# A two-layer decoder trunk on one core: the 32 loads of the first layer's scale and shift are issued by GpSimd instead of SyncE

## The reference

```python
mod = silu(c) @ w_ada + b_ada                 # c is one row of 2048; w_ada is 2048 x 6144
shift, scale, gate = split(mod, 3)
h = rmsnorm(x, norm_pre) * (1 + scale) + shift
z = h @ w_in                                  # 2048 x 14336: gb, gcin, u, g_c, q, k, v, g_r
y_conv = gb * causal_conv3(gcin * u) * silu(g_c)
q, k = rope(q, positions), rope(k, positions) * dk ** -0.5
y_ret = groupnorm(retention(q, k, v)) * gn_gain * silu(g_r)
o = concat(y_conv, y_ret) @ w_out             # 4096 x 2048
x = x + gate * rmsnorm(o, norm_post)
```

## Time and profile before

| | |
|---|---|
| median of 3 runs | 1730.23 us (1729.31 to 1730.43) |
| profiled execution | 1728.81 us, span 1727.0 us |
| TensorE busy | 1685.4 us, 98% |
| VectorE busy | 1161.1 us, 67% |
| ScalarE busy | 719.5 us, 42% |
| GpSimd busy | 51.0 us, 3% |
| moved by DMA | 429.25 MB, mean 249 GB/s |

### The profile page before, as it was taken

How to read it: one execution, slowest core, us unless ns; L and a number is a source line. 1 busy time by engine, 2 the same in 40 slices (tenths; PEclk the granted TensorE clock), 3 DMA queues, 4 the chain that set the end, 5 groups by cost and what they waited for, 6 DMA issues and landing times. The chain is left out here.

```text
span 1727.0 us, 18943 instructions
## 1 busy us (share of the span) xinstructions
PE 1685.4 (98%) x7707; PEld 1376.3 (80%) x7707; DVE 1161.1 (67%) x1296; ACT 719.5 (42%) x802; POOL 51.0 (3%) x94
## 2 busy tenths in 40 slices
PE   6999999999999999999999999999999999999997
PEld 3567878888888888778878888888888888888886
DVE  2788767788578868777776456556555654567776
ACT  3344444434444444343455444444434444444332
POOL 4000000000000000000000000000000000000000
PEclk9999999999999999999999999999999999999999
DMA  9998655787788769877775666567556756668774
GB/s 341 383 383 316 211 180 191 271 293 263 253 289 312 270 217 323 321 274 284 282 248 164 197 203 196 189 196 219 193 178 202 216 187 189 209 242 303 290 286 179
DMA packets 233655, 429.25 MB, mean 249 GB/s; under 512 B 8664, under 2 KB 50024, under 8 KB 232800
## 3 DMA queue, kind: packets, MB, share of 16 engines
q1 hardware_dynamic: 225888, 408.97, 68.5%
q10 hardware_dynamic: 7680, 19.07, 4.0%
HBM read 417.57 MB, written 2.10 MB: 243 GB/s over the span
## 5 line engine op out<-in xcount | busy, mean ns | idle before, releaser
L809 DVE TENSOR_TENSOR w_lo<-stage,w_hi 128x1024 fp32r<-128x1024 f32 x574 | 692.9, 1223 | 467.2 <-ACT w_hi L588 464.5
L588 ACT CAST w_hi<-stage 128x1024 fp32r<-128x1024 f32 x574 | 595.7, 1051 | 945.6 <-PE Z L1275 576.2
L1273 PE MATMUL Z<-w_hi,H 128*128 128x512 f32 x1784 | 702.6, 394 | 11.0 <-DVE w_lo L809 6.4
L1275 PE MATMUL Z<-w_hi,H 128*128 128x512 f32 x1784 | 695.6, 390 | 0.0
L1274 PE MATMUL Z<-w_lo,H 128*128 128x512 f32 x1784 | 695.1, 390 | 0.0
L1273 PEld LDWEIGHTS Z<-w_hi,H 128*128 128x128 f32 x1784 | 335.3, 188 | 88.9 <-issue 8.0
L1275 PEld LDWEIGHTS Z<-w_hi,H 128*128 128x128 f32 x1784 | 335.3, 188 | 70.7
L1274 PEld LDWEIGHTS Z<-w_lo,H 128*128 128x128 f32 x1784 | 335.5, 188 | 67.9
L830 DVE SCALAR_TENSOR_TENSOR acc<-stage,c_silu,acc 128x512 f32<-128x512 f32 x240 | 180.2, 751 | 6.8
L1273 PE MATMUL Z<-w_hi,YR 128*128 128x512 f32 x256 | 100.2, 391 | 2.8 <-DVE w_lo L809 2.8
L1273 PE MATMUL Z<-w_hi,YC 128*128 128x512 f32 x256 | 99.7, 389 | 0.0
(11 more groups left out here) (160 smaller groups left out, 735.0 us busy)
## 6 DMA issues: line engine op xcount, KB each, us to landing
stage<-in_w_in SPq DMA_DIRECT2D x186, 1024.0 KB, 5.2
stage<-in_w_ada SPq DMA_DIRECT2D x64, 1024.0 KB, 7.4
stage<-in_w_out SPq DMA_DIRECT2D x64, 1024.0 KB, 7.4
stage<-in_w_in SPq DMA_DIRECT2D x74, 512.0 KB, 5.6
front_stage<-in_w_ada SPq DMA_DIRECT2D x32, 1024.0 KB, 11.2
behind<-R ACTq DMA_DIRECT2D x14, 448.0 KB, 3.5
taps<-in_conv_w ACTq DMA_DIRECT2D x18, 256.0 KB, 6.5
xt<-in_x SPq DMA_DIRECT2D x2, 1024.0 KB, 6.7
```

The source lines that it names most:

```text
L588: N.copy(w_bufs(n, h)[0], stage[:, slot_of(n), 2 * h:2 * h + 2, :]).then_inc(s_hi, 1)
L809: V.tensor_tensor(lo, stage[:, slot_of(n), 2 * h:2 * h + 2, :], hi.bitcast(F32), ALU.subtract)\
L1273: T.matmul(z[:, i, :], hh, wh, start=ch.first and a == 0, stop=False)
L1275: ins = T.matmul(z[:, i, :], hl, wh, start=False, stop=stop)
```

## The change

GpSimd issues the 32 front loads on its own queue, by a new function `front_loads(upto)`, which issues the front loads up to a number, each when its slot is free. It is called at three points of GpSimd's program: for the first 4 at the start, for the next 8 after the first 1/rms, and for the other 20 after the angles. SyncE skips them in its list. Tiles, sizes, slots, semaphores and the instructions of the other engines are the same.

```diff
             for what in LOADS:
                 kind, n, kc = what
-                ring, i = RINGS[kind == "front"], PLACE[what]
+                if kind == "front":
+                    continue
+                ring, i = RINGS[False], PLACE[what]
                 slot = i % SLOTS
                 if i >= SLOTS:
                     was, m, k = ring[i - SLOTS]
                     if was == "w":
                         sp.wait_ge(s_lo, HALVES[m + 1])
-                    elif was == "front":
-                        sp.wait_ge(s_fv if on_vector(m, k) else s_front, front_done(m, k))
...
-                if kind == "front":
-                    k0, tiles = FRONT_GROUPS[n // 2]
-                    at, rows_ = front_rows_of(n, kc)
-                    col = (1 - n % 2) * D + k0 * P
-                    src = w_ada[0, at * P:(at + rows_) * P, col:col + tiles * P].rearrange("(a p) n -> p a n", p=P)
-                    sp.dma_start(front_tile(n, kc)[0], src).then_inc(s_fstage[slot], 16)
-                elif kind == "ada":
+                if kind == "ada":
...
+            def front_loads(upto):
+
+                for i in range(loaded[0], upto):
+                    _, n, kc = RINGS[True][i]
+                    if i >= SLOTS:
+                        _, m, k = RINGS[True][i - SLOTS]
+                        pool.wait_ge(s_fv if on_vector(m, k) else s_front, front_done(m, k))
+                    k0, tiles = FRONT_GROUPS[n // 2]
+                    at, rows_ = front_rows_of(n, kc)
+                    col = (1 - n % 2) * D + k0 * P
+                    src = w_ada[0, at * P:(at + rows_) * P, col:col + tiles * P].rearrange("(a p) n -> p a n", p=P)
+                    pool.dma_start(front_tile(n, kc)[0], src).then_inc(s_fstage[i % SLOTS], 16)
+                loaded[0] = upto
+
+            loaded = [0]
+            front_loads(SLOTS)
             step(G.memset(mhalf[:, :], -0.5))
             rstd(1, slice(NT, 2 * NT))
+            front_loads(3 * SLOTS)
             ang, u, m = (wide(R2)[:, i * NT * HALF:(i + 1) * NT * HALF] for i in range(3))
             pool.wait_ge(s_pos, 16 * NT)
             pool.wait_ge(s_par, 16 * 10)
...
             step(G.tensor_scalar(ang, ang, edge, None, ALU.min))
             step(G.tensor_scalar(ang, ang, -edge, None, ALU.max))
             pool.sem_inc(s_ang, 1)
+            front_loads(len(RINGS[True]))
             pool.wait_ge(s_sin, 2)
```

## The result

| | before | after |
|---|---|---|
| median | 1730.33 us (4 runs, 1729.31 to 1731.41) | 1745.9 us (4 runs, 1744.35 to 1747.43) |
| ratio after to before | | 1.0091, 95% interval 1.0076 to 1.0106 |
| profiled execution | 1728.81 us, span 1727.0 | 1746.72 us, span 1744.9 |

A forecast was written before the change was run, and what follows sets the result against it. TensorE is busy 98%; in the front, 30 to 114 us, the DMA engines are full. The 13th front tile's delay, +16.6, less 4.2 and 0.7 us, gives +11.7; median 1741.9, stated as 1741, range 1734 to 1749 us.

The forecast's parts named there:

- The start, +2 us: First product, at 30.08 us before: weight loads in flight beside the first front tiles delay it by 2 us.
- The angle block on the path: GpSimd's 32 angle instructions, 21.1 us plus 2 us stretching, run before the 13th front load and delay it.
- The issue, 0.5 us: GpSimd's issue of the 12th front load before the angle block, taken at SyncE's median of 0.518 us.
- The landing, 5.8 us: The 13th front load, issued at 72.1 us after the angles, lands 5.8 us later, at 77.9.
- f12 16.6 us late: TensorE multiplies the 13th front tile, at 61.30 us before, only when it lands at 77.9: 16.6 us late.
- What is given back, 4.9 us: TensorE's earlier idle time shrinks after the stall: 4.2 us back in 61 to 92 us, 0.7 in 92 to 114.
- The low clock, 0 us: The low-clock stretch at 92 us, costing 1.7 us, moves behind the new stall at the same price: 0.
- The steady part, 0 us: Front stretch: weight loads running ahead and front tiles coming later cancel, 0, bounds -7.0 and +5.5 us.
- The cosine step: GpSimd's cosine step, now after the last front load, has tables ready about 155 us, needed at 190.03: no cost.
- The faster one: Rival: weight loads freed from 47 us of front waits save 8.7 us, giving 1721.5 us; chance 0.07.
- The issue of 4.1 us: Rival: each front load costs GpSimd 4.1 us to issue, giving 1749 us; chance 0.10 beyond 1748.
- That the queues do nothing new: Rival: all loads share the same 16 DMA engines, so without the angle block no stall; no chance given.

The follow-up runs named there:

- kernel 6: The kernel before with only the first four front loads issued by GpSimd, the other 28 by SyncE: 1730.88 us against 1730.79.
- kernel 2: The changed kernel with GpSimd issuing only the first 12 front loads and SyncE the other 20 as before: 1731.21 us against 1730.26 for the kernel before.
- kernels 3 and 4: The changed kernel with one round of the angle reduction instead of three, 1736.92 us, and with six rounds, 1762.58 us; kernel before 1730.26.
- kernel 12: The changed kernel without the 27 instructions of the angle reduction, the other 5 before the first 1/rms: 1732.47 us against 1731.02 for the kernel before.
- Kernel 5: The changed kernel with 32 unused TensorE products before the wait for the 13th front tile: 1745.42 us against 1730.79 for the kernel before.
- kernels 1: The changed kernel with the 32 angle instructions spread behind the 8th to 13th front load: 1732.91 us against 1730.26 for the kernel before.
- kernel 7: The changed kernel, seven angle instructions before the first 1/rms, others spread behind the 8th to 12th load, first weight load waiting for the second front tile: 1732.22 us, ratio 1.0011.
- 8: The changed kernel, seven angle instructions before the first 1/rms, others spread behind the 8th to 12th load, no added weight-load wait: 1733.21 us against 1730.79 before.
- kernels 9 and 11: The changed kernel, angle instructions spread, SyncE keeping its old front-slot waits: 1734.63 us; also with weight loads waiting for the second front tile: 1736.12; kernel before 1730.38.

## Why the prediction held, point by point

*What bounds the kernel.* Right: the front, and in it the DMA engines. TensorE's idle time after 180 us is the same in both kernels (18.4 and 18.5 us). But the lateness was not settled at 114 us, as the prediction had it: it was 13.2 us there and 15.6 at the cosine step.

*The start, +2 us.* The first product starts at 32.33 us instead of 30.08, +2.25. That the delay enters the end only through the angle block was not tried by itself, but kernel 6, with a start 1.4 us late and no load behind the block, lost nothing.

*The angle block on the path.* Right, and the cause: kernel 2 takes the loads away from behind it and is as fast as before; kernels 3 and 4 change its length and move the time with it. It took 23.5 us; 21.1 + 2 had been taken. Behind it lay a gap of 0.60 us that I had not counted.

*The issue, 0.5 us.* An issue takes 0.75 us on GpSimd. The summary of the line (duration of an issue in ns, minimum, median and maximum, then the time to landing in us):

```profile
L1185 POOL DMA_DIRECT2D front_stage<-in_w_ada x32: 748/750/1107, 1.2 to 159.1; - x32
...
DMA to landing us min/median/max: 5.6/10.1/21.2
```

It is longer than SyncE's median of 0.518 but it is never 4.1. The end of f11's issue came at 49.84 us instead of 49.0.

*The landing, 5.8 us.* 79.61 - 73.95 = 5.66 us.

*f12 16.6 us late.* It was 18.3. The difference is 0.84 (end of f11's issue) + 0.4 (block) + 0.6 (gap) - 0.14 (landing) = 1.7 us. TensorE's idle time for it is 16.17 us, where the prediction had named 10 to 15.

*What is given back, 4.9 us.* By the front tile of 113.65 us the delay had shrunk from 18.3 to 13.2 us, so 5.1 came back, nearly what was predicted. Then it grew by 2.4 us up to the cosine step, in a stretch where nothing had been idle. This is the line from TensorE's waits between 114 and 180 us:

```profile
PE Z L1285 <- DVE part L1016: 1.7, 3, 0.7
```

So net 2.7 us were given back instead of 4.9. The prediction had closed its account at 114 us, and in the window from 114 to 180 us the loads are still being caught up with, 344 GB/s where 311 had been. Why 2.4 us are lost there was not tried by itself. It need not come from the stall: kernel 12, which has none, loses 2.1 us in the same stretch.

*The low clock, 0 us.* The stretch at a mean granted clock of 0.52 lasted 6.4 us, 3.1 us of lost clock instead of 1.7, so 1.4 us more. Kernel 5 undid most of that and is only 0.5 us less late at the cosine step, so on the end 0 was about right.

*The steady part, 0 us.* Not a gain, rather a loss of 1.4 to 2.7 us: all kernels that have the 32 loads on GpSimd and no block (1, 7, 8, 12) lose that much. It is small: it is below the 0.2% that the prediction calls the least that can be told from no change, and the lower ends of the four intervals are 1.0002 to 1.0006. Kernels 2 and 6, with 12 and 4 loads on GpSimd, lose less (ratios 1.0002 and 1.0). In kernel 12 it arises between 114 and 190 us, and the reason stays open. It is not a late issue of GpSimd at f13; kernels 9 and 11 do not settle whether it is the order of the weight loads; and the larger packets on GpSimd's queue, 8704 where SyncE's queue had 20992, were not tried by themselves. In the change itself this rest is not to be told from the block's effect.

*The sum.* In the terms of the prediction: +18.3 - 5.1 + 2.4 = +15.6 us at the cosine step, against 15.6 by the medians and 11.7 predicted. The terms that were too small are f12's delay (1.7 us) and what happens after 114 us (2.4 us, put at nothing). The profiled executions differ by 17.9. Of the other 2.3 us 1.6 are the clock near 260 us: both kernels have the same idle time of 2.51 us in TensorE's timeline there (first fence of before, second of after), but only after the change does a stretch at a low granted clock follow, 3.4 us long (last fence; before, the granted clock is 1.00 from 240 to 256 us):

```profile
244.06 0.50 PE L1273 MATMUL Z<-w_hi,H 128*128 128x512 f32 x1 [2.51 <-DVE w_lo L809]
```

```profile
259.67 0.70 PE L1285 MATMUL Z<-w_hi,H 128*128 128x512 f32 x1 [2.51 <-DVE w_lo L803]
```

```profile
259.60:263.00 3.40, 3.33 (x8) 2.65 (x9) 3.40 (x5) 0.00 (x0) 0.00 (x0) 0.53 0.27 67
```

Kernels 2 and 6, which are level with before by their medians, show it too (granted clock 0.89 from 240 to 256 us). So I take it for the spread of single executions and not for an effect of the change.

*The cosine step.* It ran at 159.84 us, and the tables are needed only some 205 us after the start; no cost, as said.

*The rivals.* The faster one (weight loads that no longer stand behind front waits) is refuted without the block as well: kernels 1, 7, 8 and 12 have the unblocked queue and no block, and none gains (1.0011 to 1.0015). The half of it that was true is that ScalarE's waits for weights fell, from 45.4 to 30.5 us between 30 and 114 us in kernel 12; nothing came of it at the end. The issue of 4.1 us did not come (0.75). That the queues do nothing new is true of the queues and misses the block. The Trainium skill ("DMA: Bandwidth & Descriptors", section "Issuing engines are not separate DMA queues") says that transfers started from different engines share the same 16 DMA engines and that a further issuing engine saves only issue time. The runs agree: 382 GB/s with one queue and at most 382 with two, from 30 to 114 us. The page "SBUF — State Buffer" of the Trainium skill ("Who interferes with whom") has VectorE, in its two-port modes, lock GpSimd out of writing descriptors. No run here shows it: GpSimd's issues took 0.75 us beside a busy VectorE and 1.1 us at most. In which mode VectorE worked beside them the rows do not say.

## What to carry to other kernels

A load that is moved to another engine's queue stands behind all work of that engine, so look at what is long there and compare it with how far ahead the loads run: here 23.5 us of arithmetic, begun at 49.8 us, stood before a tile that TensorE could use at 62.5 (kernel 2). In a stretch where the DMA engines are full, do not count idle time that TensorE had before as a store that a stall draws on for good: 5.1 us came back by 114 us here, and only 2.7 in the end. The transfer time missing at the rate of the stretch gave the loss to within 3 us in all thirteen kernels. A second queue gained nothing here, where the first already kept the DMA engines full; if loads must be on such an engine, cut its other work into portions between them (13 of the 15.6 us came back), or leave on the old queue those that come behind it (all of it came back).

## What the runs showed of the hardware

- GpSimd issues a load of 1 MB in 0.75 us with hardly any spread (0.748 least, 0.750 median); the first ones took up to 1.107 us. SyncE's took 0.367 to 4.102 us for the same tiles. No issue of GpSimd's took several us, though the DMA engines were as full.
- The same 33.56 MB were 20992 packets on SyncE's queue and 8704 on GpSimd's.
- A few small loads of ScalarE's queue came 3 us later after the change. TensorE's first instruction that needs them starts at 14.32 us; before, at 11.08 (second fence). SyncE's weight loads go out earlier too; when the first of them waits for f1 (kernel 7), it starts at 13.22:

```profile
14.32 0.72 PE L1380 MATMUL Z<-ident,R 80*128 80x80 f32 x3 [14.32 <-DMA R<-in_conv_w]
```

```profile
11.08 0.72 PE L1368 MATMUL Z<-ident,R 80*128 80x80 f32 x3 [11.08 <-DMA R<-in_conv_w]
```

- After 16.17 us of idle time TensorE worked at a mean granted clock of 0.52 (mostly at 1.2 GHz instead of 2.4) for 6.4 us; after 2.23 us of idle time it was 0.57 over 4 us. With products put in between, and 3.21 us of idle time, it was 0.73 over the same 6.4 us. The higher clock of that kernel goes with an end that is 0.5 to 1 us earlier, within the interval. After one and the same idle time of 2.51 us the granted clock fell in one execution (0.53 over 3.4 us) and stayed at 1.00 in another.
